# Down projection in 16 groups of 256 ff, each as seven block products instead of eight

## The reference

```python
    h = h + jnp.concatenate([conv_out, ret_out], axis=-1) @ w_out
    f = jnp.square(jax.nn.relu(rmsnorm(h, norm_ffn_w) @ w_up)) @ w_down
    return h + f, new_hist, new_state.astype(h.dtype)
...
    y_prompt = rmsnorm(hp[:, N_META:], norm_final_w)
    y_sample = rmsnorm(hs, norm_final_w)
```

## Time and profile before

| | before |
|---|---|
| runs | 1287.36, 1288.22, 1289.46 us |
| profiled execution | span of 1285.8 us; the page gives no other time of it |
| PE busy | 1267.7 us, 99% |
| DVE busy | 593.1 us, 46% |
| ACT busy | 328.1 us, 26% |
| POOL busy | 0.2 us |
| chain that ended last | PE 95%, DVE 2% |
| mean granted PE clock | 0.995 |

### The profile page before, as it was taken

The page is one execution under the profiler, slowest core; times in us unless marked ns, Lnnn a source line. Parts: engine busy times, 40 slices in busy tenths (PEclk is TensorE's granted clock), DMA queues, the critical chain, the costliest instruction groups (busy, mean ns, idle before and its releaser), DMA issues.

```text
span 1285.8 us, 17987 instructions
## 1 busy us (share of the span) xinstructions
PE 1267.7 (99%) x6972; PEld 1170.4 (91%) x6972; DVE 593.1 (46%) x1171; ACT 328.1 (26%) x647; POOL 0.2 (0%) x4
## 2 busy tenths in 40 slices
PE   8999999999999899999999999999999999999997
PEld 6999999999999688998998998998998998988986
DVE  7545444454456454642443443443443443443446
ACT  6332232232233211330330330330320320420433
POOL 0000000000000000000000000000000000000000
PEclk9999999999999899999999999999999999999999
DMA  6111111111112710120120120220220210220203
...
DMA packets 88339, 70.20 MB, mean 55 GB/s; under 512 B 9440, under 2 KB 73056, under 8 KB 88304
## 3 DMA queue, kind: packets, MB, share of 16 engines
...
## 4 chain that ended last, share of the span: by engine, by line
PE 95%; DVE 2%; DMA 1%; issue 1%; ACT 1%; DVEq 0%; SPq 0%; ACTq 0%
PE ps L1047 29%; PE ps L1049 29%; PE ps L1048 29%; PE ps L1054 1%; PE ps L1053 1%; DMA normw<-in_norm_ffn_w 1%; PE ps L1223 1%; PE ps L1146 1%; PE ps L1164 1%; PE ps L1163 1%; PE ps L1153 1%; PE ps L1132 1%; PE ps L1064 1%; DVE wo_lo L876 0%; DMA raw<-in_w_out 0%
## 5 line engine op out<-in xcount | busy, mean ns | idle before, releaser
L1047 PE MATMUL ps<-mid_hi,ws_hi 128*128 128x368 f32 (+1 forms) x768 | 251.3, 327 | 0.2 <-DVE ws_lo L955 0.2
L1049 PE MATMUL ps<-mid_hi,ws_lo 128*128 128x368 f32 (+1 forms) x768 | 251.4, 327 | 0.0
L1048 PE MATMUL ps<-mid_lo,ws_hi 128*128 128x368 f32 (+1 forms) x768 | 250.8, 327 | 0.0
L1047 PE MATMUL ps<-hn_hi,ws_hi 128*128 128x368 f32 (+1 forms) x648 | 219.7, 339 | 1.2 <-DVE hn_lo L724 1.2
L1048 PE MATMUL ps<-hn_lo,ws_hi 128*128 128x368 f32 (+1 forms) x648 | 213.3, 329 | 0.0
L1049 PE MATMUL ps<-hn_hi,ws_lo 128*128 128x368 f32 (+1 forms) x648 | 212.8, 328 | 0.0
L981 DVE SCALAR_TENSOR_TENSOR h<-ps,inv_ms,h 128x512 f32<-128x512 f32 (+1 forms) x144 | 108.0, 750 | 226.7 <-PE ps L1049 217.2
L1047 PE MATMUL ps<-wd_hi,f_hi 128*128 128x512 f32 x512 | 199.2, 389 | 0.0
L1048 PE MATMUL ps<-wd_lo,f_hi 128*128 128x512 f32 x512 | 199.2, 389 | 0.0
L1049 PE MATMUL ps<-wd_hi,f_lo 128*128 128x512 f32 x512 | 199.2, 389 | 0.0
L624 ACT ACTIVATE wd_hi<-raw 128x512 fp32r<-128x512 f32 x64 | 39.3, 625 | 438.8 <-PE ps L1049 438.8
...
## 6 DMA issues: line engine op xcount, KB each, us to landing
raw<-in_w_up SPq DMA_DIRECT2D x64, 256.0 KB, 3.0
raw<-in_w_down SPq DMA_DIRECT2D x64, 256.0 KB, 2.8
raw<-in_w_in SPq DMA_DIRECT2D x56, 256.0 KB, 2.9
raw<-in_w_out SPq DMA_DIRECT2D x16, 256.0 KB, 3.0
out<-hw SPq DMA_DIRECT2D x16, 256.0 KB, 2.0
...
```

Source lines behind the costliest of these rows:

```text
L1047: pe.matmul(out, a_hi, b_hi, start=start, stop=False)
L1048: pe.matmul(out, a_hi, b_lo, start=False, stop=False)
L1049: return pe.matmul(out, a_lo, b_hi, start=False, stop=stop)
```

## The change

The number of groups doubles to 16, with 256 ff (two blocks) each. In a group, the activations F are seen as 2 x 2 blocks: prompt rows 0 to 511 and 512 to 1023 (four row tiles each; quad q, 0 to 3, is the pair of row tiles q and q + 4), and the two ff blocks. The down weights B are 2 x 2 blocks too: the two ff blocks, and columns 0 to 511 and 512 to 1023. The product is formed by seven block products in place of eight, in the form with 15 additions: P1 = A11 B11, P2 = A12 B21, P3 = S4 B22, P4 = A22 T4, P5 = S1 T1, P6 = S2 T2, P7 = S3 T3, with S1 = A21 + A22, S2 = S1 - A11, S3 = A11 - A21, S4 = A12 - S2, and T1 to T4 from the B blocks in the same way. Each is 4 row tiles x 3 matmuls of 512 columns. Two banks per q are used: P1, P6, P7 and P4 accumulate in the first one without a reset, P2, and then P5 and P3, in the second. Between two of them the partial sum is taken out of the bank: P1, P2, P5 and P7 by a DVE addition to h, and P6, P4 and P3 by an ACT copy to one of four SBUF buffers `tmp` and a POOL addition to h. P1 and P2 run over all four q; P6, P5, P7, P4 and P3 first for q = 0 and 1, then for q = 2 and 3. The sample rows are still done with all eight block products' worth of matmuls.

POOL also forms T1 to T4, S3 and S4, DVE forms S1 and S2. The down weights are loaded into `dr`, which lies over hw. ReLU and square are both on ACT. The inverse root of the mean square is now applied before the up projection: ACT works it out (`rms`), and `normed_ffn` on DVE multiplies with it.

```diff
-GROUPS = 8
-FT = FF // GROUPS // P
+GROUPS = 16
...
+P1, P2, P6, P5, P7, P4, P3 = range(OPS)
...
+BANK1 = [0, 1, 2, 6]
+BANK2 = [7, 3, 4, 5]
+IN_BANK1 = [P1, P6, P7, P4]
+FRESH = [P1, P2, P5]
+H_OF = {P1: (0, 0), P2: (0, 0), P6: (0, 1), P3: (0, 1), P4: (1, 0), P5: (1, 1), P7: (1, 1)}
+ORDER = [(p, q) for p in (P1, P2) for q in range(QUADS)] \
+    + [(p, q) for pair in ((0, 1), (2, 3)) for p in (P6, P5, P7, P4, P3) for q in pair] + ["sample"]
...
+DVE_ADDS = [(p, q) for p in (P1, P2) for q in range(QUADS)] \
+    + [(p, q) for pair in ((0, 1), (2, 3)) for p in (P5, P7) for q in pair]
+POOL_ADDS = [(p, q) for pair in ((0, 1), (2, 3)) for p in (P6, P4, P3) for q in pair]
...
+            def load_down(g, first):
+                if first:
+                    sp.wait_ge(ht_done, TILES)
+                    sp.wait_ge(d_ready, len(D_LO) * g)
+                for k in range(2):
+                    for nh in range(2):
+                        src = w_down_t[:, bass.ds(g * 2 + k, 1), nh * 512:nh * 512 + 512].rearrange("p a c -> p (a c)")
+                        sp.dma_start(dr[:, k, nh, :], src).then_inc(dr_in[2 * k + nh], 16)
...
+            def rms(t):
+                n = rows(t)
+                for nh in range(2):
+                    act.wait_ge(out_taken, 2 * t + nh + 1)
+                    if t or nh:
+                        act.wait_ge(ms2_ready, 3 * t + nh)
+                    act.activation(tmp0[0:n, :], h[0:n, t, nh * 512:nh * 512 + 512], ACT.Square,
+                                   accum_out=fin[0:n, t, nh:nh + 1]).then_inc(ms2_ready, 1)
+                act.wait_ge(ms2_ready, 3 * t + 1)
+                act.activation(fin[0:n, t, 2:3], fin[0:n, t, 0:1], ACT.Identity, scale=1.0 / D, bias=eps[0:n, :]).then_inc(ms2_ready, 1)
+                act.wait_ge(ms2_ready, 3 * t + 3)
+                act.activation(fin[0:n, t, 3:4], fin[0:n, t, 1:2], ACT.Sqrt, scale=1.0 / D, bias=fin[0:n, t, 2:3]).then_inc(sd2_ready, 1)
...
+                base = NU * HEADS + 2 * g
+                act.wait_ge(prod_done, NPROD * g + 1)
+                for name in D_LO:
+                    d_hi(g, name)
+                act.wait_ge(w_used, base + 1)
+                split_ffn(g, "up", 1, 0)
+                act.wait_ge(f_ready, NLO * g + 1)
+                relu_square(g, 0, 0)
+                relu_square(g, 0, 1)
+                f_hi(g, "A11")
+                relu_square(g, 0, 2)
+                split_ffn(g, "up", 1, 1)
+                f_hi(g, "S3")
...
+                relu_square(g, 1, 0)
+                f_hi(g, "A12")
+                f_hi(g, "S2")
+                f_hi(g, "S1")
+                f_hi(g, "S4")
+                f_hi(g, "f12")
+                if not last:
+                for k in range(len(POOL_ADDS_LAST if last else POOL_ADDS)):
+                    copy_out(g, k, last)
...
+            def add(g, p, q, last):
+                dve.wait_ge(prod_done, NPROD * g + n_prod(p, q, last))
+                adds = DVE_ADDS_LAST if last else DVE_ADDS
+                same = [x for x in adds[:adds.index((p, q))] if x[1] == q and H_OF[x[0]] == H_OF[p]]
+                if same:
+                    dve.wait_ge(dve_add, NDVE * g + n_dve_add(*same[-1], last))
+                if p in (P3, P4):
+                    dve.wait_ge(pool_add, NPOOL * g + 4 + len(POOL_ADDS_LAST))
+                dve.tensor_tensor(h_part(p, q), bank_of(p, q)[:, :], h_part(p, q), ALU.add).then_inc(dve_add, 1)
...
+                add(g, P1, 0, last)
+                f_low(g, "A12")
+                add(g, P1, 1, last)
+                f_low(g, "S2")
+                add(g, P1, 2, last)
+                add(g, P1, 3, last)
+                f_low(g, "f12")
+                f_low(g, "S1")
+                for q in range(QUADS):
+                    add(g, P2, q, last)
+                f_low(g, "A22")
+                if not last:
+                f_low(g, "S4")
+                if not last:
+                    for p, q in DVE_ADDS[8:]:
+                        add(g, p, q, False)
+                    sample_add(g, False)
...
+                add(g, P5, 2, True)
+                add(g, P5, 3, True)
+                dve.wait_ge(normw_in, 32)
+                final_norm(0)
+                final_norm(1)
+                sample_add(g, True)
+                add(g, P7, 2, True)
+                add(g, P7, 3, True)
+                final_norm(2)
+                add(g, P3, 2, True)
+                add(g, P3, 3, True)
+                final_norm(3)
+                add(g, P4, 2, True)
+                add(g, P4, 3, True)
+                for p in range(4, TILES):
+                    final_norm(p)
...
+                t1, t2, t3, t4 = (do_raw[:, D_OF[name], :] for name in ("T1", "T2", "T3", "T4"))
+                pool.tensor_tensor(t1, b12, b11, ALU.subtract).then_inc(d_sum, 1)
+                pool.tensor_tensor(t3, b22, b12, ALU.subtract).then_inc(d_sum, 1)
+                pool.wait_ge(d_sum, 4 * g + 1)
+                pool.tensor_tensor(t2, b22, t1, ALU.subtract).then_inc(d_sum, 1)
+                pool.wait_ge(d_sum, 4 * g + 3)
+                pool.tensor_tensor(t4, b21, t2, ALU.subtract).then_inc(d_sum, 1)
+                pool.wait_ge(fr_ready, 6 * g + 3)
+                pool.tensor_tensor(fo_raw[:, P7, :], fr[:, 0, 0:512], fr[:, 0, 512:1024], ALU.subtract).then_inc(f_sum_pool, 1)
+                pool.wait_ge(fr_ready, 6 * g + 6)
+                pool.wait_ge(f_sum_dve, 3 * g + 2)
+                pool.tensor_tensor(fo_raw[:, P3, :], fr[:, 1, 0:512], fr[:, 0, 512:1024], ALU.subtract).then_inc(f_sum_pool, 1)
+                adds = POOL_ADDS_LAST if last else POOL_ADDS
+                for k, (p, q) in enumerate(adds):
+                    pool.wait_ge(act_copy, NPOOL * g + k + 1)
+                    same = [x for x in adds[:k] if x[1] == q and H_OF[x[0]] == H_OF[p]]
+                    if same:
+                        pool.wait_ge(pool_add, NPOOL * g + n_pool_add(*same[-1], last) + 4)
+                    pool.tensor_tensor(h_part(p, q), tmp(k, last), h_part(p, q), ALU.add).then_inc(pool_add, 1)
...
+            def product(g, p, q, first, last_group):
+                if q % 2 == 0:
+                    name = {i: x for x, i in F_OF.items()}[p]
+                    pe.wait_ge(f_ready, NLO * g + F_LO.index(name) + 2)
+                    name = {i: x for x, i in D_OF.items()}[p]
+                    pe.wait_ge(d_ready, len(D_LO) * g + D_LO.index(name) + 1)
+                if p == P1:
+                    if q < 3:
+                        pe.wait_ge(relu_done, 6 * g + q + 1)
+                    elif not first:
+                        pe.wait_ge(samp_add, 4 * g)
+                elif p == P2:
+                    if q > 0:
+                        pe.wait_ge(relu_done, 6 * g + 3 + UP_ORDER[1].index(q - 1) + 1)
+                    elif not first:
+                        pe.wait_ge(samp_add, 4 * g)
+                elif p == P6:
+                    pe.wait_ge(dve_add, NDVE * g + n_dve_add(P1, q, last_group))
+                elif p == P5:
+                    pe.wait_ge(dve_add, NDVE * g + n_dve_add(P2, q, last_group))
+                elif p == P7:
+                    pe.wait_ge(act_copy, NPOOL * g + n_pool_add(P6, q, last_group))
+                elif p == P4:
+                    pe.wait_ge(dve_add, NDVE * g + n_dve_add(P7, q, last_group))
+                else:
+                    pe.wait_ge(dve_add, NDVE * g + n_dve_add(P5, q, last_group))
+                at = q * P
+                passes(bank_of(p, q)[:, :], fo_hi[:, p, at:at + P], fo_lo[:, p, at:at + P], do_hi[:, p, :], do_lo[:, p, :],
+                       start=p in FRESH, stop=True, again=p not in FRESH).then_inc(prod_done, 1)
```

More of the change, by code:

```diff
@@ L674, in _ @@
+                if last:
+                    for p in range(5):
+                        final_early(p)
+                        final_late(p)
+                    for p in range(5, TILES):
+                        final_early(p)
+                    for p in range(5, TILES):
+                        final_late(p)
             with act.Fori(0, GROUPS - 1) as g:
@@ L1313, with group @@
+            def group(g, first, last_group):
+                up(g, first)
+                for step in ORDER_LAST if last_group else ORDER:
+                    if step == "sample":
+                        sample(g, last_group)
+                    else:
+                        product(g, *step, first, last_group)
+            group(0, True, False)
+            with pe.Fori(1, GROUPS - 1) as g:
+                group(g, False, False)
+            group(GROUPS - 1, False, True)
 _INS = ["x_prompt", "x_sample", "state_conv", "state_ret", "meta_tokens", "norm_mix_w", "w_in", "conv_w", "ret_gn_w",
```

462 lines of the change are left out of this document (278 added, 184 removed).

## The result

The changed kernel takes 1389.08 us (median of 4 runs, 1387.19 to 1390.47) where the kernel before, in the same session, takes 1287.79. The ratio is 1.079, with a 95% interval of 1.0774 to 1.0806. The forecast was 1314.5: the direction was right, the size was not, 26 us forecast against 101 measured. The profiled run has a span of 1385.4 us.

What follows compares the result with a forecast made beforehand. PE, 99% busy, was taken to bound the kernel. Products -43.5, start +10.3, waits 15 x 2.9 and last group +15.9 sum to +26.2: a span of 1312, 1314.5 as a median, range 1303 to 1326.

Steps and rivals of the forecast that it cites:

- Products: Seven block products for eight: a group takes 44.53 us, 2.72 less than 47.25; 16 groups save 43.5.
- Wait inside a group: PE waits before P4 for DVE's P7 addition: 2.46 idle, 0.27 in the second pair, restarts; 2.9 us per group.
- the 15 operations: DVE's wide operations from A12's low part to the P7 addition of quad 0, 0.61 us apart, needing 9.3.
- A: DVE operations with two SBUF inputs wait for running POOL additions; 16 x 1.5 = 24 us, time 1339; chance 0.25.
- B: Idle gaps drop PE's clock in each group; 15 x 1.7 = 25 us, time 1340; chance 0.07.
- Rival C: In each group P4 finds its P7 addition done, so no stall; -17.3 us, time 1271; chance 0.14.
- the chance of faster: Chance that the changed kernel is faster than the one before: 0.14; same 0.04, slower 0.82.
- Rival D: Waits before every third matmul themselves cost PE 28 x 0.05 per group, 22 us, time 1337; chance 0.05.
- Start and last group: First group: PE waits for the sample tile and weight split, 10.3; last group: additions and norms finish late, 15.9.
- the 17.9: Last group, last matmul to end of span: products end at 49.3, norms near 63.7, span at 67.2.
- The signs: Trace after: PE about 95% busy, P4 wait 2 to 3 us, start idle 5 to 9, end some 14.

Runs made afterwards that it cites:

- e7: Changed kernel with DVE's order by need, second up block split before the down weights, S4 after A12's low part, P3 before P4, sample banks moved: 1271.21 us.
- e12: Changed kernel with four added 512-column matmuls on PE before P4 of quad 0 in each looped group: 1373.47 us.
- e10: Changed kernel with the second up block's split ahead of the down weights' on ACT and DVE, and its loads ahead in group 0: 1371.43 us.
- e3: Changed kernel without POOL's twelve additions to h in each group, DVE's order unchanged: 1334.18 us.

## Why the prediction was right or wrong

- **Products, -43.5.** Right. Without idle on PE a group takes 44.83 (e7) where 44.53 was forecast; 0.3 x 16 = 5 us off.
- **Wait inside a group, 15 x 2.9.** This is the step that failed. Its mechanism was right (P4 on the P7 addition, DVE without a gap from A12 on), its price was not: 52.3 - 44.53 = 7.8 us a group where 2.9 was forecast. Per group, against the forecast: the pace 0.1; the P4 wait 0.94 (POOL's additions add 1.53 and S4 beside A12's low part 0.6, but PE comes to P4 0.8 late after its stop before P2, and the idle in the row starts 0.16 late; the 15 operations themselves were counted right); two stops that I had not looked for, before P2 (0.55, A12's low part beside S4) and on the split (0.30, POOL's sums late in ACT's and DVE's order); the stops themselves 4 x 0.26 where I took 2 x 0.1, from a row in which I had read only the second half of the cost; and the clock, 2.0 on average. Together 4.8 of the 4.9.
- **Rivals A and B.** Both were named, sized about right, and both are true. I had given each a chance as if the other were absent, and a forecast without either. But A lengthens the very idle on which B depends, so they belonged in one case: 1314.5 + 24 + 25 is already 1364. B was thought unlikely at 0.07 since 2.5 us lay between an idle that dropped the clock and one that did not; e12 says that 2.5 does it in two groups of three.
- **Rival C, and the chance of faster.** Wrong for this kernel, as DVE's queue was indeed too long. Its time of 1271 is what e7 reaches once the order is mended, the tail still as it was. That the numbers agree so closely is luck in part: e7's loop is 5 us dearer than C's, and its start cheaper.
- **Rival D.** Refuted by e7, and by starts 0.2267 apart in the changed kernel.
- **Start and last group, 10.3 and 15.9.** Right as a sum, to some 3 us, and partly by luck. The span grew by 99.6 us where 26.2 was forecast, 73.4 more, and the fifteen looped groups account for 15 x 4.9 = 73. But the profiled run after comes to its first up matmul 3.1 us earlier than the one before (517.4 against 520.5), mostly because a wait ahead of the ff part is 3.19 and not the 5.42 of the earlier trace rows; that wait scatters from 2.6 (e10) to 7.1 us (e3) between runs whose code up to there is the same, so start and end cost some 3 more than forecast. Singly: 9.57 of idle for 6.9 (within the 5 to 10), 4.96 for 4.1, and 15.6 for 17.9 from the last matmul to the end. In the 17.9 some 0.7 came from a misread row: 1282.35 is where the first of the two products in the earlier trace rows ends, the last one ends at 1283.01.
- **The signs.** PE's share was to be 95% and is 92%, the wait before P4 2 to 3 us and is 3.4, the idle on the split 5 to 9 and is 9.57. The end was to take some 14 us, which does not fit the 17.9 of the prediction's own sum, and took 15.6. DVE has one gap between the first P1 addition and the first P7 addition, 0.29 before A12's low part. The signs of rivals A and B came as written: low parts of 1.13 to 1.76 beside POOL, and a granted clock of 0.50 within groups.

That the clock dropped for eight matmuls in some groups and fourteen in others was only observed; what decides between them stays open, and likewise which of the equal idles of e3 and e12 drop it. The length alone does not: in e3 an idle of 2.10 left the clock alone and one of 1.85 dropped it.
